# A hybrid attention layer: output turn by transposes with the halves folded on VectorE, three query tiles in one block each, compression inside the projection

## The reference, cut to what matters

```python
h = rmsnorm(x, norm_mix_g);  proj = h @ w_in          # x: 1024 tokens x 1024, w_in: 1024 x 2840
q, k_c, v_c, k_s, v_s, k_w, v_w, g_lin, b_g, c_g, u = split(proj)    # 8 query heads, 2 key heads, 64 wide
k_cmp = gelu(blocks(k_c + pos) @ w_ck1) @ w_ck2       # 63 blocks of 32 tokens at stride 16; v_cmp alike
o_attn = sum over 3 branches of gate * softmax(q k^T - alibi, masked) v
         # compressed keys | selected blocks (here 16 of 16: all earlier keys) | a window of 512 keys
o_conv = b_g * causal_dwconv(c_g * u)
x = x + concat(rmsnorm(o_attn), rmsnorm(o_conv)) @ w_out
h2 = rmsnorm(x);  x = x + (silu(causal_dwconv(h2 @ w_gate) + b) * (h2 @ w_up)) @ w_down
return rmsnorm(x)
```

## Time and profile before

| | us |
|---|---|
| median of 3 runs | 1413.08 (1412.99 to 1414.23) |
| profiled execution, its own time | 1413.54 |
| its span, first to last instruction | 1411.7 |
| the first projection ends at about | 272.5 |
| first score matmul | 288.57 |
| the last matmul of attention with values ends at about | 607.3 |

### The profile page before, as it was taken

How to read it: one execution, slowest core, us unless ns; L and a number is a source line. 1 busy time by engine, 2 the same in 40 slices (tenths; PEclk the granted TensorE clock), 3 DMA queues, 4 the chain that set the end, 5 groups by cost and what they waited for, 6 DMA issues and landing times.

```text
span 1411.7 us, 17432 instructions
## 1 busy us (share of the span) xinstructions
PE 1356.0 (96%) x6574; PEld 1098.8 (78%) x6574; DVE 854.2 (61%) x1183; ACT 561.1 (40%) x1044; POOL 293.5 (21%) x193
## 2 busy tenths in 40 slices
PE   7999999989999999989997999999999999999996
PEld 6788888867777777768886788888888878888885
DVE  6433342358777777655357977777778873335542
ACT  6212111267666766533164333333333333234330
POOL 0100100201011100000045654544555410002010
PEclk9999999989999999999998999999999999999998
DMA  5111121000000000043212112221222238444631
GB/s 217 52 45 46 59 59 76 19 1 16 1 1 1 1 1 1 1 179 120 74 45 83 67 60 90 90 82 68 91 90 90 75 115 318 149 138 147 211 101 60
DMA packets 37918, 110.80 MB, mean 78 GB/s; under 512 B 3988, under 2 KB 4500, under 8 KB 37652
## 3 DMA queue, kind: packets, MB, share of 16 engines
q1 hardware_dynamic: 37552, 108.86, 22.1%
q0 software_dynamic: 288, 0.90, 0.4%
HBM read 90.05 MB, written 19.92 MB: 78 GB/s over the span
## 4 chain that ended last, share of the span: by engine, by line
PE 77%; DVE 12%; issue 6%; ACT 4%; DMA 1%; POOL 1%; DVEq 0%; SPq 0%; ACTq 0%; POOLq 0%
PE PS L465 9%; PE PS L466 8%; PE PS L469 8%; PE PS L1942 6%; PE PS L1944 6%; PE PS L1943 6%; PE PS L1954 6%; PE PS L1956 6%; PE PS L1955 6%; PE PS L1812 3%; DVE wl L1488 3%; PE PS L1839 2%; PE PS L1768 2%; PE PS L1828 2%; PE PS L1769 2%
## 5 line engine op out<-in xcount | busy, mean ns | idle before, releaser
L465 PE MATMUL PS<-R,wh 128*128 128x512 f32 x560 | 221.6, 396 | 12.7 <-DVE wl L457 12.7
L466 PE MATMUL PS<-R,wh 128*128 128x512 f32 x560 | 219.2, 391 | 0.0
L1942 PE MATMUL PS<-R,wh 128*128 128x512 f32 x480 | 189.5, 395 | 14.0 <-DVE wl L1488 8.4
L1943 PE MATMUL PS<-R,wh 128*128 128x512 f32 x480 | 188.2, 392 | 0.0
L1944 PE MATMUL PS<-R,wl 128*128 128x512 f32 x480 | 188.0, 392 | 0.0
L469 PE MATMUL PS<-R,wl 128*128 128x512 f32 x560 | 173.3, 391 | 0.0
L1954 PE MATMUL PS<-R,wh 128*128 128x512 f32 x352 | 137.5, 390 | 0.0
L1956 PE MATMUL PS<-R,wl 128*128 128x512 f32 x352 | 137.0, 389 | 0.0
L1955 PE MATMUL PS<-R,wh 128*128 128x512 f32 x352 | 137.0, 389 | 0.0
L465 PEld LDWEIGHTS PS<-R,wh 128*128 128x128 f32 x560 | 106.0, 189 | 36.5 <-DVE wl L457 13.6
L986 ACT ACTIVATE F<-PS,nmax 128x64 f32<-128x64 f32 (+6 forms) x192 | 108.4, 570 | 44.1 <-DVE nmax L1362 43.3
(11 more groups left out here) (216 smaller groups left out, 2379.5 us busy)
## 6 DMA issues: line engine op xcount, KB each, us to landing
raw<-in_w_units SPq DMA_DIRECT2D x70, 512.0 KB, 3.7
F<-in_w_units SPq DMA_DIRECT2D x32, 512.0 KB, 4.1
gated<-F SPq DMA_DIRECT2D x22, 512.0 KB, 2.6
F<-gated SPq DMA_DIRECT2D x44, 256.0 KB, 3.6
F<-in_xT SPq DMA_DIRECT2D x16, 512.0 KB, 9.2
F<-in_w_units SPq DMA_DIRECT2D x12, 384.0 KB, 3.2
residual<-F SPq DMA_DIRECT2D x8, 512.0 KB, 2.6
F<-residual SPq DMA_DIRECT2D x8, 512.0 KB, 6.5
```

The costliest lines, as they stand in the source:

```text
L465: nc.tensor.matmul(out, w_h, hi(kt)[:, cols], start=first, stop=False)
L466: nc.tensor.matmul(out, w_h, lo(kt)[:, cols], start=False, stop=False)
L1942: nc.tensor.matmul(out, w_h, operand(name, k, 0), start=fresh and k == 0, stop=False, skip_group_check=not fresh)
L1943: nc.tensor.matmul(out, w_h, operand(name, k, 1), start=False, stop=False, skip_group_check=not fresh)
```

## The change

**Turn.** `turn_out` becomes four transposes of 128 columns against the identity. The halves are then still apart in PSUM, and VectorE adds them (`add_halves`, a reduction over pairs of 512 elements to 256). GpSimd weighs each group (`weigh`, one multiplication per group) and adds the branches. The turn comes six steps behind a group instead of five, the squares ten instead of eight.

**Blocks.** Query tiles 0, 1 and 2 of each key head have one block with all three branches (`KEYS_OF_ALL`): 26 blocks and 104 units instead of 32 and 128. Steps and groups stay at 148 and 48. Tile 0 has its compressed keys first.

**Row sums.** The compressed branch's exponential no longer writes a row sum; VectorE sums its 4 x 64 exponentials once per query tile.

**Plain steps.** None before block 9: the copy's buffer `EP` now lies in the keys of the second head. 33 instead of 49.

**Compression.** The two hidden layers run behind units 20 and 21, and the first `w2c` product behind them, so unit 22 is TensorE's last piece before attention. After it come the turn of the first head's values and the scores.

**Preparation.** Keys are laid out in halves of 512 tokens, the later ones between units; only query head 0 before the first scores. GpSimd makes both copies of the even heads' later queries. The second head's values are turned in two pieces at steps 30 and 33. A small `Exp` on ScalarE stands before the end of the projection. All eight loads of the residual input follow the end of attention (one of them was earlier).

```diff
-CMP_FIRST = [i not in (0, 3, 7) for i in range(TT)]
+CMP_FIRST = [i < SMALL or i not in (3, 7) for i in range(TT)]
...
-BLOCKS = [(g, i, kind) for g in range(KV) for i in range(TT) for kind in range(2)]
+BLOCKS = [(g, i, kind) for g in range(KV) for i in range(TT)
+          for kind in ([KEYS_OF_ALL] if i < SMALL else [KEYS_OF_SEL, KEYS_OF_WIN])]
...
-PV_LAG, COPY_LAG, TURN_LAG, SQUARE_LAG = 2, 3, 5, 8
+PV_LAG, COPY_LAG, TURN_LAG, SQUARE_LAG = 2, 3, 6, 10
...
-PLAIN = [s_plain % 3 == 1 for s_plain in range(NS)]
+KEYS_DONE = 34
+PLAIN = [n_plain > KEYS_DONE // GROUP and s_plain % 3 == 1 for s_plain, (n_plain, _, _, _) in enumerate(STEPS)]
...
-KEYS_AT = {26: 0, 30: 1}
+KEYS_AT = {8: (0, 0, 1), 11: (0, 1, 1), 23: (1, 0, 0), 26: (1, 1, 0), 29: (1, 0, 1), 32: (1, 1, 1)}
... GpSimd
+            def weigh(group):
+                pool.wait_ge(t_used, O_OF[group] + 1)
+                pool.wait_ge(coef_ready, n + 1)
+                nc.gpsimd.tensor_tensor(heads(part(br)), heads(part(br)), factor[...].broadcast_to([P, GROUP, DH]), ALU.mult)
+                if br == order[1]:
+                    nc.gpsimd.tensor_tensor(part(order[0]), part(order[0]), part(br), ALU.add).then_inc(o_step, 1)
+                if br == order[2]:
+                    nc.gpsimd.tensor_tensor(F1[...], part(order[0]), part(br), ALU.add).then_inc(o_ready, 1)
... ScalarE
-                    last = nc.scalar.activation(e, pair(U % 2)[:, col:col + count], ACT.Exp, bias=nmax[:, br, i, h:h + 1],
-                                                accum_out=den[:, i % 2, br * GROUP + h:br * GROUP + h + 1])
+                    total = {} if br == CMP else {"accum_out": den[:, i % 2, br * GROUP + h:br * GROUP + h + 1]}
+                    last = nc.scalar.activation(e, pair(U % 2)[:, col:col + count], ACT.Exp, bias=nmax[:, br, i, h:h + 1], **total)
... VectorE
+                if CMP in [br for m, br, _, _ in GROUPS if m == n]:
+                    nc.vector.tensor_reduce(den[:, i % 2, CMP * GROUP:(CMP + 1) * GROUP], E_C[:, i % 2, :, :], AX.X, ALU.add)
...
-                nc.vector.tensor_tensor(OS[:, i % 2, br, :], PS[:, 4 + at % 2, 0:GROUP * DH], factor[...], ALU.mult)
+                nc.vector.tensor_reduce(OS[:, i % 2, br, :].rearrange("p (h d) -> p h d", d=DH),
+                                        PS[:, 4 + at % 2, :].rearrange("p (h e d) -> p h d e", e=2, d=DH), AX.X, ALU.add)
... TensorE
             for n in range(14, N_IN):
                 unit_matmuls(pe, n, 0, 0, 0, n % 3, h_hi, h_lo)
+                if n == 20:
+                    compressed_hidden(0, range(CMP_BLOCK // 2))
+                if n == 21:
+                    compressed_hidden(1, range(CMP_BLOCK // 2))
...
                 for h in range(GROUP):
-                    last = nc.tensor.matmul(PS[:, 4 + at % 2, h * DH:(h + 1) * DH], OT[group % 2][:, h * P:(h + 1) * P], fold,
-                                            start=True, stop=True)
+                    last = nc.tensor.transpose(PS[:, 4 + at % 2, h * P:(h + 1) * P], OT[group % 2][:, h * P:(h + 1) * P], ident)
```

More of the change, by code:

```diff
@@ L245, in hybrid_layer @@
         RF = R1[:, :, :].rearrange("p a b -> p (a b)")
+        KEY_ORDER = [(0, 0, 0), (0, 1, 0)] + [KEYS_AT[U] for U in sorted(KEYS_AT)]
+        KEYS_BEFORE = 2
         KCMP, KSEL, KWIN, KEYS = 0, CW, CW + T, CW + 2 * T
@@ L762, in _, with query_tiles, queries_again, queries @@
             pool.wait_ge(unit_done, N_IN)
+            def query_tiles(g, half, h):
+                tiles = slice(half * TT // 2, (half + 1) * TT // 2)
+                return tiles, F1[0:DH, Q0 + 2 * g + h // 2, :].rearrange("p (i q) -> p i q", q=P)[:, tiles, :]
+            def queries_again(g, half, h):
+                tiles, src = query_tiles(g, half, h)
+                nc.gpsimd.tensor_scalar(QB[0:DH, tiles, h, :], src, DH ** -0.5, None, ALU.mult).then_inc(qb_even, 1)
+            def queries(g, half, h):
+                tiles, src = query_tiles(g, half, h)
+                if g:
+                    pool.wait_ge(sc_ready, FREE_Q[1 + half])
+                nc.gpsimd.tensor_scalar(QA[0:DH, tiles, h, :], src, DH ** -0.5, None, ALU.mult).then_inc(qp_hi, 1)
+                queries_again(g, half, h)
@@ L778, in _ @@
[L778 to L791 removed]
+            queries_again(0, 0, 2)
@@ L925, in _, with keys @@
             split_hi(act, 22, 0, 0, 0)
-            def keys(g, half):
-                rows = slice(half * DH, (half + 1) * DH)
-                nc.scalar.activation(KA[g][rows, KSEL + half * T:KSEL + (half + 1) * T], F1[rows, K0 + 2 * g, :], ACT.Copy)\
-                    .then_inc(k_hi, 1)
+            def keys(g, half, part):
+                rows, cols = slice(half * DH, (half + 1) * DH), slice(part * BANK, (part + 1) * BANK)
+                nc.scalar.activation(KA[g][rows, KSEL + half * T:KSEL + (half + 1) * T][:, cols], F1[rows, K0 + 2 * g, cols],
+                                     ACT.Copy).then_inc(k_hi, 1)
             def queries(g, half, h):
@@ L959, in compressed_values @@
                         .then_inc(vc_hi, 1)
-            act.wait_ge(unit_done, N_IN)
-            act.wait_ge(qkv_ready, 8)
-            for half in range(2):
-                keys(0, half)
-            for h in range(GROUP):
-                queries(0, 0, h)
-            hidden(0)
-            values_hi(0)
-            hidden(1)
+            for kv in range(2):
+                hidden(kv)
             act.wait_ge(kvc_ready, 1)
@@ L973, in _ @@
             act.wait_ge(kcs_ready, 1)
+            nc.scalar.activation(den[0:DH, 0, 0:1], kcs[:, 0, 0:1], ACT.Exp)
+            act.wait_ge(unit_done, N_IN)
+            for half in range(2):
+                keys(0, half, 0)
+            queries(0, 0, 0)
             compressed_keys(0)
+            for h in range(1, GROUP):
+                queries(0, 0, h)
+            values_hi()
             def exponentials(U):
@@ L1349, in _ @@
             for half in range(2):
-                keys(0, half)
-            position_bias(0)
-            for h in range(GROUP):
-                queries(0, 0, h)
-            position_bias(1)
+                keys(0, half, 0)
+            queries(0, 0, 0)
+            compressed_keys(0)
             def row_max(U):
@@ L1782, in scores @@
                 cmp_mask, lead = M_CMP + i * CW, CW * CMP_FIRST[i]
-                if kind == 0:
+                if kind != KEYS_OF_WIN:
                     diag = lead + i * P
                     run(KSEL - lead, lead + P * (i + 1), [0, diag] if lead else [diag])
+                    if kind == KEYS_OF_ALL:
+                        part(bank + 1, 0, KWIN, P * (i + 1), True)
                     if lead:
@@ L1788, in scores @@
                     last = mask(diag, M_DIAG, P)
+                    if kind == KEYS_OF_ALL:
+                        last = mask(BANK + i * P, M_DIAG, P)
                 else:
@@ L1824, in values @@
                     pe.wait_ge(vc_lo, KV)
+                if s == first and ROWS[n] == TT:
+                    pe.wait_ge(t_used, V_OF[VALUES_AT[-1]] + 1)
                 rows = slice(0, NCMP if br == CMP else P)
@@ L1838, in turn_out, with turn_values @@
                 for h in range(GROUP):
-                    last = nc.tensor.matmul(PS[:, 4 + at % 2, h * DH:(h + 1) * DH], OT[group % 2][:, h * P:(h + 1) * P], fold,
-                                            start=True, stop=True)
+                    last = nc.tensor.transpose(PS[:, 4 + at % 2, h * P:(h + 1) * P], OT[group % 2][:, h * P:(h + 1) * P], ident)
+                last.then_inc(tr_ready, 1)
+            def turn_values(s):
+                at = V_OF[s]
+                pe.wait_ge(t_used, at - 1)
+                for t in range(HALF_T):
+                    tile = HALF_T * VALUES_AT.index(s) + t
+                    last = nc.tensor.transpose(PS[:, 4 + at % 2, t * P:(t + 1) * P], F1[:, V0 + 2, tile * P:(tile + 1) * P], ident)
                 last.then_inc(tr_ready, 1)
```

322 lines of the change are left out of this document (175 added, 147 removed).

## The result

The changed kernel takes **1433.5 us** (median; 1432.1 to 1433.8) against 1413.0 for the kernel before. The ratio is 1.014, 95% interval [1.012, 1.016]. The change makes the kernel slower by about 20 us; forecast were 1398 us, in a range up to 1416. The profiled execution has a span of 1430.3 us, 18.6 more than before.

A forecast was written before the change was run, and what follows sets the result against it. TensorE was taken to set the pace, VectorE next. Terms of -20.7 - 5.0 - 2 + 8 + 4.1 + 0.7 = -14.9 us gave 1398 us; 1391 to 1407 by its own bounds, range 1384 to 1416.

The forecast's parts named there:

- I count nothing for it: Attention: ScalarE's 16 more high parts, less 64 accumulator reads, priced at nothing because it has 98 us idle.
- signs of being wrong: Reduction over 0.9 us, GpSimd multiplications above 1.5, stretch under 275 or over 292 us, clock under 1.00 behind 315 us.
- Turn, -20.7 us on TensorE: Attention: four transposes take 0.44 us where a turn took 0.89; 46 turns at 0.45 us saved each.
- Plain steps, -5.0 us: Attention: 16 plain steps become split ones, each saving TensorE 0.31 us.
- Fewer units, -2 us: Small query tiles: 24 hand-overs between the three engines go, saving 2 us, between 0 and 12.5.
- VectorE, +8 us, 0 to 15.4: Attention from 310 us: longer reductions and row sums on VectorE, under an 84.5% busy ceiling, give back 8 us.
- Start, +4.1 us, 0 to 6.1: Start of attention: with the hidden layer's cover gone, scores wait for a DMA; attention starts 4.1 us later.
- The clock, one fall, nothing counted: Start of attention: one clock fall again, as before, so no cost; a second would cost up to 5 us.
- the rule of the Trainium skill: Attention: transposes do not count as busy for the clock gate like other matmuls, so the clock would fall again.
- End, +0.7 us: End of attention: the last two groups' extra GpSimd and VectorE work adds 0.7 us, 0 to 1.6.
- VectorE becomes the bound: Rival, from 310 us on: VectorE limits attention and the kernel is slower, 1416 to 1422 us; chance 0.14.
- The clock falls inside attention: Rival: falls of 10 us cost up to 5 us each; three take the gain, 1413 us; chance 0.05.

The follow-up runs named there:

- b_turn: The kernel before with the new turn alone (four transposes, halves added on VectorE, weighing on GpSimd; turn still five steps behind): 1406.2 us.
- a_plain: The changed kernel with every third step plain from the first one on: 1426.8 us.
- b_turn_split: b_turn with none of the first 49 steps plain, so 16 plain steps become split ones: 1406.5 us.
- a_best_small0: a_best with the first three query tiles split into two blocks each again, as before the change: 1415.3 us.
- b_turn_lag610: b_turn with the change's longer lags, turn 6 and squares 10 steps behind instead of 5 and 8: 1413.6 us.
- a_order: The changed kernel with ScalarE's high part of the later values moved ahead of its step and exponentials: 1426.5 us.
- a_best: Changed kernel with value high parts first, every third step plain, all queries before scores, row sum on ScalarE, hidden layer back, lags 5 and 9: 1408.4 us.

## Why the prediction was wrong, step by step

The forecast was -14.9 us and the measurement +20.4. What failed is the pricing of the work beside TensorE by how long its engine idles: the prediction's "I count nothing for it" for ScalarE, the start held to 6.1 us at most, and no term at all for the lags and for the place of the value pieces. Two of the signs of being wrong came: the clock fell inside attention behind 315 us, and the stretch from 310 us to the end of attention, 297.3 us before, is 315.

- **Turn, -20.7 us on TensorE.** The durations were right: 0.44 us less for each turn in b_turn, against 0.45; the reduction 0.68; GpSimd's weighing 0.61. With all of VectorE's +8, which also held the row sums, I had a net of -12.7 for it; measured are -6.8. TensorE's whole busy time fell by 14.8 us only, and it waits more; the 6 us between that and the turns' 21.0 are not assigned to any line.
- **Plain steps, -5.0 us.** Wrong in sign in the changed kernel: there plain steps are worth 6.6 us (a_plain), on b_turn nothing (b_turn_split). I counted nothing for ScalarE and for the hop from ScalarE to VectorE, since both idle. In a chain that waits for both, that hop is the likely price (argued, not measured by itself); 0.31 us of TensorE is not the gain. That the price depends on how tight the rest is, I did not have at all.
- **Fewer units, -2 us.** Right in sign, undersized: 7 us (a_best_small0), inside its own bound of 12.5.
- **VectorE, +8 us, 0 to 15.4.** Priced by its busy share, with a ceiling of 84.5%. That is the step of the method that failed, on both sides. The share is no ceiling: in b_turn VectorE is busy 94% of these 10 us, with TensorE at 92%, and the kernel is faster than before.

```profile
330.00:340.00 10.00, 9.21 (x61) 6.80 (x60) 9.44 (x18) 7.45 (x21) 2.60 (x5) 1.00 0.00 0
```

And in after, where it reached only 77% over the stretch, the kernel is slower. Its cost comes by position: 0.41 us of row sum, 16 times, with a wait behind it, cost 4 us.

- **Start, +4.1 us, 0 to 6.1.** The first scores were forecast to 0.1 us (293.8, measured 293.94), in part by luck: the projection ended some 0.8 us earlier than I had it, and the scores came 7.0 us behind it, not 6.1. The first exponential came at 296.01, where I had 295.2. The step that failed is the next sentence, "VectorE and ScalarE have nothing but the remaining preparation": that preparation was moved behind the first row maxima and released the next three units. The first tile was 9.2 us late, and putting the hidden layer back was worth 10.6 us.
- **The clock, one fall, nothing counted.** In the kernel before TensorE did not mostly wait ahead of the fall: read in steps of 2 us, it was busy 3.5 of the 6 us from 290 to 296. In after the low level at the start lasted 17 us, not 10, and there are five more behind 330 us, four of them in the first head's tiles and each behind a wait. In b_turn, with all 192 new transposes, it is 0.99 from 310 to 607.3 us. That is one fall of some 3 us, which the kernel before does not have, and the longest wait in the 10 us ahead of it is 0.73 us:

```profile
450.00:460.00 10.00, 8.80 (x51) 6.38 (x50) 7.34 (x25) 8.25 (x35) 1.07 (x1) 0.83 0.00 1
```

In b_turn_lag610, with the same transposes, it is 1.00 from 310 to 607.3 us. So the transposes do not bring it down by themselves; whether they had a part in that one fall is not shown. That bears against the rule of the Trainium skill, "TensorE: Matmul & The Clock Gate", Part 4, as I used it for a rival: transposes stand in both kernels more densely than before, and the level holds nearly throughout.
- **Lags, no term.** 4 to 7 us, read over in the diff as a constant.
- **Value pieces, no term for ScalarE's order.** 7 us (a_order).
- **End, +0.7 us.** From the last split matmul with values to the output projection's matmul behind the wait are 10.2 us (625.07 to 635.26) where 10.0 were before (606.94 to 616.92): +0.2, inside its bounds.

Of the rivals, none was right as a whole. "VectorE becomes the bound" gave 1416 to 1422 with the right sign and the wrong reason. "The clock falls inside attention" named something that happened: there were more short waits, and five falls. But by the estimate above they cost some 9 us of the 35 between forecast and measurement, and they followed the waits. Errors of one sign came together: in every part I priced engines and not the places in their queues.

The parts, measured one at a time: turn -7 and merging -7 on one side; values' order 7, plain steps 7, queries 4 (together 12), row sum 4, hidden layer 11 and lag 6 on the other. That makes 19 of the 20.4 us, but the sum proves little, as the parts do not add: all repairs together brought 25 us (1433.5 to 1408.4) and not 33. What is left without a name is the 9 us by which a_best stands above the kernel before with turn and merging taken off.

## What to carry to other kernels

Where three engines hand a step on in a ring, work that leaves the busiest one comes back only as far as the waits allow; price each moved instruction by what stands behind it in its own queue, and ask whether its engine meets a wait there that another engine ends. Read every constant of a schedule (a lag, a number of buffers) as a wait: a lag longer by one step can want a buffer more. And what looks like preparation to be hidden somewhere needs a long block of independent work above it; when the change moves that block, look at the second and third unit, not only at the first.

## What was not expected of the hardware

- A reduction over 512 elements of PSUM takes VectorE 684 to 688 ns whether it leaves one result or 256.
- TensorE's clock fell to the 1.2 GHz level inside attention after waits of 1.5 to 3.5 us (after: 2.38 us ahead of 333.24, 1.88 ahead of 367.50, 3.46 ahead of 392.10, 2.27 ahead of 420.38, 1.51 ahead of 494.47), for some 3 to 4 us each. Waits of 1.94 and 1.75 us ahead of 379.71 and 383.42 brought no fall (1.00 over 380 to 390 us). So a wait can cost more than its length, and here its length alone did not tell whether it would.
- VectorE was busy 94% of a stretch of 10 us while TensorE was busy 92% (b_turn, 330 to 340 us).
